# A hybrid recurrent, attention and expert layer: other forms and places for its normalizations

## The reference

```python
def _rmsnorm(x, w):
    y = xf * lax.rsqrt(jnp.mean(xf * xf, axis=-1, keepdims=True) + EPS)
    return (y * w.astype(jnp.float32)).astype(x.dtype)
...
    log_a = -RGLRU_C * r.astype(f32) * jax.nn.softplus(-lam.astype(f32))
    a = jnp.exp(log_a)
    b = jnp.sqrt(-jnp.expm1(2.0 * log_a)) * (i * xc).astype(f32)
...
    _, h = lax.associative_scan(combine, (a, b), axis=1)
    return (h * jax.nn.gelu(gate.astype(f32))).astype(u.dtype)
...
    q = _rmsnorm(q.reshape(B, S, N_HEADS, HEAD_DIM), q_norm_w).astype(f32)
    k = _rmsnorm(k.reshape(B, S, N_HEADS, HEAD_DIM), k_norm_w).astype(f32)
...
        mix = jnp.concatenate([_rmsnorm(rec, rec_out_norm_w[l]).astype(x.dtype),
                               _rmsnorm(att, attn_out_norm_w[l]).astype(x.dtype)], axis=-1)
        x = x + jnp.einsum('bse,ed->bsd', mix, w_out[l])
        x = x + _moe(_rmsnorm(x, ln2_w[l]), w_router[l], b_router[l], w_gate_up[l], b_gate_up[l],
                     w_down[l], b_down[l])
```

## Time and profile before

| | us |
|---|---|
| median of 3 runs | 2202.7 |
| lowest and highest | 2198.86 and 2208.48 |
| the profiled execution | 2205.51 |
| its span in the trace | 2203.7 |
| PE busy in the span | 2004.5 |
| DVE busy | 1343.1 |
| ACT busy | 1043.5 |
| POOL busy | 392.7 |

### The profile page before, as it was taken

The page is one execution under the profiler, slowest core; times in us unless marked ns, Lnnn a source line. Parts: engine busy times, 40 slices in busy tenths (PEclk is TensorE's granted clock), DMA queues, the critical chain, the costliest instruction groups (busy, mean ns, idle before and its releaser), DMA issues.

```text
span 2203.7 us, 50552 instructions
## 1 busy us (share of the span) xinstructions
PE 2004.5 (91%) x20393; PEld 1832.2 (83%) x20393; DVE 1343.1 (61%) x2592; ACT 1043.5 (47%) x1432; POOL 392.7 (18%) x297
## 2 busy tenths in 40 slices
PE   6998899997597489999999999999999999998993
PEld 4776676775486279999999999999999999998883
DVE  4678834453523865555566665677586777767572
ACT  4463213444211144544555555665565656565561
POOL 3000000000000211111112112131233333324231
PEclk9999899996797689999999999999999999999996
DMA  4111100001142757888888999999999999999993
GB/s 130 48 39 29 29 10 10 20 20 51 39 172 104 278 187 270 283 282 282 291 278 283 301 309 316 339 295 331 340 357 373 366 363 372 356 371 352 369 355 109
DMA packets 251768, 501.77 MB, mean 228 GB/s; under 512 B 13024, under 2 KB 33808, under 8 KB 251584
## 3 DMA queue, kind: packets, MB, share of 16 engines
q1 hardware_dynamic: 231376, 446.73, 55.9%
q0 software_dynamic: 20256, 51.73, 10.8%
q10 hardware_dynamic: 48, 2.10, 0.3%
HBM read 471.16 MB, written 52.43 MB: 238 GB/s over the span
## 4 chain that ended last, share of the span: by engine, by line
PE 50%; DMA 5%; DVE 4%; issue 3%; SPq 1%; ACT 1%; POOL 0%; DVEq 0%; ACTq 0%; POOLq 0%
PE E_p_d L1667 21%; DMA E_w_st<-in_w_down 5%; PE E_p_g L1656 4%; PE E_p_g L1658 4%; PE E_p_g L1659 4%; PE E_p_u L1656 4%; PE E_p_u L1658 4%; PE E_p_u L1659 4%; DVE E_w_lo L1497 2%; PE E_p_t L1638 2%; PE E_p_t L1623 2%; SPq L1306 1%; ACT E_w_hi L1420 1%; DVE E_up L1557 0%; DVE E_gate L1545 0%
## 5 line engine op out<-in xcount | busy, mean ns | idle before, releaser
L1497 DVE SCALAR_TENSOR_TENSOR E_w_lo<-E_w_st,E_w_hi 128x2048 f16<-128x2048 f32 x260 | 594.7, 2287 | 61.8 <-ACT E_w_hi L1420 58.1
L1420 ACT ACTIVATE E_w_hi<-E_w_st 128x2048 f16<-128x2048 f32 x260 | 492.6, 1905 | 191.9 <-PE E_p_g L1659 103.2
L1667 PE MATMUL E_p_d<-E_a_f,E_w_st 128*128 128x160 f32 (+6 forms) x4096 | 537.2, 291 | 24.1 <-DMA E_w_st<-in_w_down 17.6
L1667 PEld LDWEIGHTS E_p_d<-E_a_f,E_w_st 128*128 128x128 f32 x4096 | 522.1, 193 | 31.6 <-DMA E_w_st<-in_w_down 19.0
L1656 PE MATMUL E_p_g<-E_x_hi,E_w_hi 128*128 128x160 f16 (+6 forms) x2048 | 373.0, 224 | 9.6 <-issue 9.6
L1656 PE MATMUL E_p_u<-E_x_hi,E_w_hi 128*128 128x160 f16 (+6 forms) x2048 | 371.7, 223 | 5.0 <-DVE E_w_lo L1497 5.0
L1658 PE MATMUL E_p_g<-E_x_lo,E_w_hi 128*128 128x160 f16 (+6 forms) x2048 | 373.0, 224 | 0.0
L1659 PE MATMUL E_p_g<-E_x_hi,E_w_lo 128*128 128x160 f16 (+6 forms) x2048 | 372.9, 224 | 0.0
L1658 PE MATMUL E_p_u<-E_x_lo,E_w_hi 128*128 128x160 f16 (+6 forms) x2048 | 371.7, 223 | 0.0
L1659 PE MATMUL E_p_u<-E_x_hi,E_w_lo 128*128 128x160 f16 (+6 forms) x2048 | 371.6, 223 | 0.0
L1369 POOL DMA_INDIRECT sum_rows<-E_y_rows,E_idx_out x66 | 169.3, 2566 | 606.0 <-ACT E_y_rows L1438 595.9
(11 more groups left out here) (338 smaller groups left out, 3053.0 us busy)
## 6 DMA issues: line engine op xcount, KB each, us to landing
E_w_st<-in_w_gate_up SPq DMA_DIRECT2D x130, 2048.0 KB, 14.9
E_w_st<-in_w_down SPq DMA_DIRECT2D x64, 2048.0 KB
A_w_st<-in_w_in SPq DMA_DIRECT2D x20, 512.0 KB, 3.8
sum_rows<-C_x SPq DMA_DIRECT2D x10, 512.0 KB, 5.8
A_x_rows<-in_x SPq DMA_DIRECT2D x8, 512.0 KB, 8.0
B_wo_st<-in_w_out SPq DMA_DIRECT2D x8, 512.0 KB, 3.1
C_x_res<-in_x SPq DMA_DIRECT2D x8, 512.0 KB, 4.2
x_rows<-C_x SPq DMA_DIRECT2D x8, 512.0 KB, 5.0
```

Source lines behind the costliest of these rows:

```text
L1420: act.activation(w_hi[c % RI][:], staged(c % NG), ACT.Copy, scale=SW).then_inc(hi_s, 1)
L1497: dve.scalar_tensor_tensor(out=w_lo[c % RI][:], in0=staged(c % NG), scalar=SW, in1=w_hi[c % RI][:], op0=ALU.mult, op1=ALU.subtract, accum_ ...
L1667: ins = pe.matmul(banks[:, h, 0:w], staged(c)[:, k, h * P:(h + 1) * P], x[:, k, 0:w], start=h == 0 and k == 0, stop=k == KT - 1, skip_grou ...
```

## The change

- **Recurrence.** 1 − a² is computed as (a² + 1) · t: ACT adds a Square of `decay` into `denom` behind the tanh, and DVE does one product of two operations in place of the addition, reciprocal and product.
- **q and k.** The means of all eight tiles are accumulated into 16 rows of one PSUM tile (`head_cols`, whose window moves with j, so that each product fills two of 16 rows and adds zero to the others). One addition, one reciprocal and one root on 16×1024 follow after the last. The root is split into three bf16 parts (`rs_b`), which PE spreads over 128 partitions by a table `head_rows` (`spread_root`), two tiles behind each of V's row tiles 3 to 6; DVE multiplies q and k by them straight from PSUM. POOL fills the two tables after the last gates.
- **rec.** Its squares, means, reciprocal, root and scaling move from stage C into A: squares on ACT at q/k tiles 1 to 4, `rec_squares` on PE behind projections 10 to 13, the reciprocal on DVE at n = 13, the root on ACT at tile 6, the scaling on DVE at n = 15.
- **att.** The sums of squares of att move into stage B, behind head 5 of the next row block, the last one to B's end.
- The forget gates' arithmetic moves up to n = 8 to 10.

The diff, cut to its core:

```diff
+            pool.wait_ge(rg_mm, CT)
+            step(pool.memset(rs_b[:], 0.0))
+            step(pool.memset(head_rows[:], 0.0))
...
                 act.activation(rgate[:], rgate[:], ACT.Tanh, scale=decay_pos[:, c:c + 1]).then_inc(tanh_s, 1)
+                act.activation(denom[:], decay[:], ACT.Square).then_inc(tanh_s, 1)
                 act.wait_ge(var_s, c + 1)
                 act.activation(denom[:], denom[:], ACT.Sqrt).then_inc(sqrt_s, 1)
...
-                    act.activation(square[:], m.qk[:, j, :], ACT.Square).then_inc(act_step, 1)
-                    step.n += 1
+                    act.activation(square[:], m.qk[:, j, :], ACT.Square).then_inc(sq_s, 1)
                     if j == 0:
                         recur(CT - 1)
-                    else:
-                        act.wait_ge(ms_s, j)
-                        act.activation(rscale[:], rscale[:], ACT.Sqrt).then_inc(rs_s, 1)
+                    elif j <= CT:
+                        if j == 1:
+                            act.wait_ge(rec_s, CT)
+                        if j > 1:
+                            act.wait_ge(rec_mm, j - 1)
+                        act.activation(rec_sq[:], m.rec[:, j - 1, :], ACT.Square).then_inc(rec_sq_s, 1)
+                    if j == 1:
+                        act.wait_ge(lam_abs, 2)
+                        act.activation(zexp, zabs, ACT.Exp, scale=-1.0).then_inc(lam_exp, 1)
+                    elif j == 2:
+                        act.wait_ge(lam_one, 2)
+                        act.activation(zlog, zone, ACT.Ln).then_inc(lam_log, 1)
+                    elif j == 6:
+                        act.wait_ge(rec_ms, 1)
+                        act.activation(rec_rs[:], rec_rs[:], ACT.Sqrt).then_inc(rec_root, 1)
             for n in (18, 19):
                 split_hi(n)
-            act.wait_ge(ms_s, 8)
-            act.activation(rscale[:], rscale[:], ACT.Sqrt).then_inc(rs_s, 1)
-            act.wait_ge(lam_abs, 2)
-            act.activation(zexp, zabs, ACT.Exp, scale=-1.0).then_inc(lam_exp, 1)
-            act.wait_ge(lam_one, 2)
-            act.activation(zlog, zone, ACT.Ln).then_inc(lam_log, 1)
+            act.wait_ge(tables, 1)
+            act.wait_ge(ms_s, 1)
+            act.activation(rs[:], rs[:], ACT.Sqrt).then_inc(rs_s, 1)
+            act.wait_ge(rs_s, 1)
+            act.activation(rs_b[0:NR, :], rs[:], ACT.Copy).then_inc(hi_s, 1)
+            act.wait_ge(rest_s, 1)
+            act.activation(rs_b[32:32 + NR, :], rs[:], ACT.Copy).then_inc(mid_s, 1)
             for t in range(T):
                 act.wait_ge(v_mm, t + 1)
                 act.activation(m.v[:, t, :], p_in[(t // 2) % 2][:, t % 2, :], ACT.Copy).then_inc(v_act, 1)
@@ -400,13 +432,10 @@
             dve.tensor_scalar(decay_neg, z[:, 0:CT], -8.0, None, ALU.mult).then_inc(lam_s, 1)
             def norm_qk(j):
 
...
-                dve.wait_ge(tanh_s, c + 1)
-                step(dve.tensor_scalar(denom[:], rgate[:], 1.0, None, ALU.add))
-                step(dve.reciprocal(denom[:], denom[:]))
-                dve.scalar_tensor_tensor(out=denom[:], in0=rgate[:], scalar=2.0, in1=denom[:],
-                                         op0=ALU.mult, op1=ALU.mult).then_inc(var_s, 1)
+                dve.wait_ge(tanh_s, 2 * c + 2)
+                dve.scalar_tensor_tensor(out=denom[:], in0=denom[:], scalar=1.0, in1=rgate[:],
+                                         op0=ALU.add, op1=ALU.mult).then_inc(var_s, 1)
...
-                elif n > 8:
-                    norm_qk(n - 9)
+                    dve.wait_ge(z_s, 1)
+                    step(dve.tensor_scalar(zdiff, z, -1.0, None, ALU.mult))
+                    dve.tensor_tensor(zabs, zdiff, z, ALU.max).then_inc(lam_abs, 1)
+                    step(dve.tensor_scalar(z, z, 0.0, None, ALU.min))
+                elif n == 10:
+                    log1p_exp(T * H, 2)
+                    step(dve.tensor_tensor(m.logf[:], z, zlog, ALU.subtract))
+                elif n == 13:
+                    dve.wait_ge(rec_mm, CT)
+                    step(dve.tensor_scalar(rec_rs[:], p_g[1][:].rearrange("p a b -> p (a b)"), EPS, None, ALU.add))
+                    dve.reciprocal(rec_rs[:], rec_rs[:]).then_inc(rec_ms, 1)
+                elif n == 15:
+                    dve.wait_ge(rec_root, 1)
+                    for c in range(CT):
+                        step(dve.scalar_tensor_tensor(out=m.rec[:, c, :], in0=m.rec[:, c, :], scalar=rec_w[:, c:c + 1],
+                                                      in1=rec_rs[:], op0=ALU.mult, op1=ALU.mult))
             split_lo(18)
             split_lo(19)
-            norm_qk(7)
-
-            dve.wait_ge(z_s, 1)
-            step(dve.tensor_scalar(zdiff, z, -1.0, None, ALU.mult))
-            dve.tensor_tensor(zabs, zdiff, z, ALU.max).then_inc(lam_abs, 1)
-            step(dve.tensor_scalar(z, z, 0.0, None, ALU.min))
-            log1p_exp(T * H, 2)
-            step(dve.tensor_tensor(m.logf[:], z, zlog, ALU.subtract))
+            dve.wait_ge(ms_mm, 2 * CT)
+            step(dve.tensor_scalar(rs[:], p_g[0][0:NR].rearrange("p a b -> p (a b)"), EPS, None, ALU.add))
+            dve.reciprocal(rs[:], rs[:]).then_inc(ms_s, 1)
+            dve.wait_ge(hi_s, 1)
+            dve.tensor_tensor(rs[:], rs[:], rs_b[0:NR, :], ALU.subtract).then_inc(rest_s, 1)
+            dve.wait_ge(mid_s, 1)
+            dve.tensor_tensor(rs_b[64:64 + NR, :], rs[:], rs_b[32:32 + NR, :], ALU.subtract).then_inc(rest_s, 1)
+            for j in range(2 * CT):
+                norm_qk(j)
 
         @block.tensor
         def _(pe):
@@ -502,20 +544,37 @@
                         pe.wait_ge(u_s if q % 2 == 0 else gelu_s, q // 2 + 1)
                     else:
                         pe.wait_ge(qk_s, q - 7)
-                        pe.wait_ge(act_step, CT + q - 7)
                 for half in range(2):
...
             def mean_squares(j):
-                pe.wait_ge(act_step, CT + j + 1)
-                if j:
-                    pe.wait_ge(ms_s, j)
+                pe.wait_ge(sq_s, j + 1)
+                if j == 0:
+                    pe.wait_ge(sig_s, 2 * CT)
                 for half in range(2):
-                    ins = pe.matmul(p_g[0][:, half, :], m.head_ones[:], square[:, half * 512:(half + 1) * 512],
-                                    start=True, stop=True)
+                    ins = pe.matmul(p_g[0][0:NR, half, :], m.head_cols[:, NR - 2 - 2 * j:2 * NR - 2 - 2 * j],
+                                    square[:, half * 512:(half + 1) * 512], start=j == 0, stop=j == 2 * CT - 1)
                 ins.then_inc(ms_mm, 1)
+
+            def rec_squares(c):
+                pe.wait_ge(rec_sq_s, c + 1)
+                for half in range(2):
+                    ins = pe.matmul(p_g[1][:, half, :], m.rec_ones[:], rec_sq[:, half * 512:(half + 1) * 512],
+                                    start=c == 0, stop=c == CT - 1)
+                ins.then_inc(rec_mm, 1)
+
+            def spread_root(j):
+                if j == 0:
+                    pe.wait_ge(rest_s, 2)
+                    pe.wait_ge(rec_ms, 1)
+                if j >= 2:
+                    pe.wait_ge(qkn_s, j - 1)
+                for half in range(2):
+                    ins = pe.matmul(p_g[(j + 1) % 2][:, half, :], head_rows[:, j, :],
+                                    rs_b[:, half * 512:(half + 1) * 512], start=True, stop=True)
+                ins.then_inc(rs_mm, 1)
...
+                if 10 <= n < 10 + CT:
+                    rec_squares(n - 10)
...
+                if 3 <= t < 7:
+                    spread_root(2 * t - 6)
+                    spread_root(2 * t - 5)
...
+                if h == 5 and n // H:
+                    row_squares(n // H - 1)
+            row_squares(T - 1)
...
-            for t in range(T):
-                if t:
-                    act.wait_ge(att_sq, t)
-                act.activation(bin_[:], m.att[:, t, :], ACT.Square, accum_out=att_ss[:, t:t + 1]).then_inc(att_sq, 1)
-            for c in range(CT):
-                if c:
-                    act.wait_ge(ms_mm, c)
-                act.activation(rec_sq[:], m.rec[:, c, :], ACT.Square).then_inc(sq_s, 1)
             act.wait_ge(att_pre, 1)
             act.activation(att_rs, att_ss, ACT.Sqrt).then_inc(att_ok, 1)
-            act.wait_ge(rs_pre, 2)
-            act.activation(rec_rs[:], rec_rs[:], ACT.Sqrt).then_inc(rs_ok, 1)
             for g in range(CT):
-                act.wait_ge(rec_n, g + 1)
                 act.activation(mix_hi[:, g, :], m.rec[:, g, :], ACT.Copy).then_inc(mix_hi_s, 1)
             for g in range(2 * CT):
                 c, half = g % CT, g // CT
```

76 lines of the change are left out of this document (38 added, 38 removed).

## The result

The changed kernel takes 2169.97 us (median of 4 executions, 2163.18 to 2173.13) against 2202.26 us (4 executions) before; the ratio is 0.9846, with a 95% interval of 0.9813 to 0.9879. The profiled execution took 2168.48 us with a span of 2166.7 us, 37.0 us less than the span of before; the forecast for it was 37.5 us less. The medians differ by 32.3 us.

A forecast was written before the change was run, and what follows sets the result against it. Stage A was taken as bound by PE with two pauses, C's head by an ACT, DVE and PE chain; 4.7 us in A plus 32.8 in C, 37.5 us, took the median 2202.7 to 2165.2 us, range 2157 to 2175.

The forecast's parts named there:

- First pause: Stage A, PE's 6.87 us wait until 188.88: it goes, with the slow clock behind it, saving 10.1 us.
- the thinning: Last recurrence in stage A without add, reciprocal and one product: rec complete at 173.6 us, not 179.89.
- Narrow head means cost as much as wide: Stage A: head means with 16 output columns cost the same as with 128; products start 0.23 us apart.
- Rec means in A: Four pairs of f32 products moved into stage A, 1.73 us each, cost PE 6.9 us.
- Second pause: Stage A, PE's 8.57 us wait before V: V starts at 262.0 instead of 270.33, scalings of rec last.
- Root of q and k: Stage A beside V: ready at about 276, hidden by 9 us; sixteen spread products add 3.6 us to PE.
- rival 1: Last recurrence in A: POOL's selects and DVE take turns, rec slips up to 16.6 us; 2165 to 2176; chance 0.13.
- rival 2: Stage B: att's sums of squares delay ACT's exp and PE, 5.7 us, 2170.9; chance 0.06.
- rival 3: Early in B: the 1.2 GHz stretch goes (2160) or comes once more (2170); chance 0.06 to each side.
- Rival 4: B's dense rows, 352 to 515 us, held at 1.2 GHz: slower than before, up to 2328; chance 0.02.
- Head of C: Start of stage C: first low half of rec at 540.35 instead of 573.11, saving 32.75 us.
- rival 5: Head of C: chain held by something not seen, PE's turns or loads; 8 us allowed, 2173; chance 0.03.

The follow-up runs named there:

- again: The changed kernel run once more with no edit: 2176.18 us, ratio 0.9886.
- wide: The changed kernel with head means by weights of 128 columns instead of 16: 2170.60 us, ratio 0.9855.
- wide_late: The changed kernel with 128-column head means and the four scalings of rec moved from in front of V to beside V: 2166.64 us, ratio 0.985.
- before_again: The kernel before run once more with no edit: 2208.59 us, ratio 1.0025.
- c_head_back: The changed kernel with the norm of rec and att's sums of squares back at the head of stage C: 2196.41 us, ratio 0.998.

## Why the forecast held, step by step

**The whole.** On the same clock the gain is 35.5 us, not 37.5: 33.05 in C where the forecast had 32.75, and in A 6.64 − 4.16 = 2.5 where it had 4.7. In the two profiled executions C's first projection came 32.4 us earlier: these 35.7 (412.83 − 377.11), less 2.6 us for a longer stretch at 1.2 GHz in B, less 0.8 us since this execution reached the first head means later. From there to the end it was 4.7 us shorter than the one before (1613.5 for 1618.1), where no instruction was changed. The same program as before, profiled again, took 1614.9 there, so most of that is chance, and with it the spans differ by 37.0, as if the forecast had been right to half a us. The median, 2169.97, sits inside the range, 4.8 us above the forecast; that of `again`, 2176.18, is outside it by 1.2 us.

**First pause: right,** V aside. Both pairs run at once, at full clock, with no pause. The forecast put the gain down to the wait that goes, listed the thinning apart, and did not ask what either does alone; the runs say 9.35 us for the thinning by itself and nothing for it on top. Its remark that a shorter recurrence alone buys nothing holds up to 182 us only, not for the pause behind.

**Narrow head means cost as much as wide: wrong,** the only term of the sum that failed in its reason. The forecast took it from products with 8 columns 0.23 us apart, a stream of narrow products only, where no wide load follows. Between wide projections it is 0.3 us a pair, 12.95 for 12.65 (and 14.64, not 14.4, with the rec means), and `wide` says that it puts V 1.7 us later. That closes the account: 8.3 us forecast, 101.13 − 94.49 = 6.6 found.

**Rec means in A: right.** 14.64 − 12.95 = 1.69 us a pair against 1.73.

**Second pause: right in its order.** The idle 2.20 us in front of the last means (2.4 forecast), the scalings last (5.24 us against 5.0), and `wide_late` gained 2.7 us by moving them, twice the 1.3 that the forecast gave for it. For the time without them the forecast had put both low halves behind ACT's second high half; the first of them runs beside it.

**Root of q and k: right.** 6.54 us for 16 partitions, as for 128; the asking 10 us behind the end. From V to the start of B 4.16 us were added, not 3.6: the spread products themselves 3.6 by their spacing, and the hand-over of stages 0.45 us more (2.22 against 1.77).

**POOL, rival 1.** Its mechanism is there, its price was wrong. Three selects took 4.56 us, not 16.6 (the row below), so only the igate product stood beside them; and with six times as many DVE lost 1.56 us up to rec.

```profile
161.32 4.56 POOL L225 TENSOR_SCALAR_AFFINE_SELECT A_head_rows<-A_head_rows 32x1024 bf16<-32x1024 bf16 x3
```

**B's sums, rival 2: excluded** for one sum each, and with a reason the forecast did not have: in the long row blocks there would be room for three.

**The clock, rival 3: the mechanism right, its size wrong.** The forecast allowed 5 us either way, from one profile. The two programs show 3.6 to 17.4 us, kernels with the same B down to 0, and the profile of before happened to be the mild one at 3.6. The range held the first median because it had to hold other rivals too, and it did not hold that of `again`.

**Rival 4** did not happen: the hold of 37.6 us in `again` and `before_again` is of its kind, but it ended by itself, and it came to both kernels alike. That nothing else in the trace showed such a hold was not so: the kernel before ran at 1.2 GHz from 515.9 to 550.0 us, with PE busy for 9.57 of the 10 us from 520 to 530.

**Head of C: right,** and rival 5 excluded. 33.05 us against 32.75, up to the first low half and up to the first projection alike, so nothing unseen held the chain; `c_head_back` gives it back.

## What to carry to other kernels

A chain of squares, means, roots and scalings at the head of a stage, where every engine but one idles, can be dissolved into the stages before it. Here that took 33 us out of the head and cost 9.3 us in stage A (6.8 us of PE for the means, the rest for the scalings), which leaves 23 of the 35.5 us. Before crediting two removals in one queue with two gains, ask what each leaves for the other: here either one alone clears the pause but for half a us. And when medians wander by 10 us, measure the trace from point to point, take out the stretch that the clock disturbs, and compare the rest: that told versions apart by 2 us which their times could not.

## What the hardware showed that was not expected

- Products of f32 with weights of 16 or 32 columns between products with 128: their loads are not made ahead, nor is the first wide one behind them; 12.95 us against 12.65 for a projection and its pair, though each load takes 0.10 and not 0.19 us.
- A stretch at 1.2 GHz with PE busy throughout (16.00 of 16 us at a granted clock of 0.50) lasted 10.2 or 37.6 us in two executions of the kernel before and 13.7 or 37.6 us in two of the changed kernel, and in two other kernels with the same stage B it was absent. It began 22 to 25 us behind the start of B in each of the ten profiles that show it, at or behind the end of the forget sums, where PE pauses 0.26 us in every 2.53 us (it is busy for 16.08 of the 18 us from 318). The Trainium skill, "TensorE: Matmul & The Clock Gate", section "A second HAM failure mode: psum-queue depth-cycling", describes a kernel in which frequent short pauses between groups of products make the clock go down and up; the place of the fall agrees with that, the one fall that then holds for 37.6 us with PE busy does not, and the two runs with filled gaps did not decide it.
- DVE and POOL take turns instruction by instruction: a POOL select of 1.13 us took up to 2.93 us beside DVE, and a DVE step of 0.18 us took 1.13.
